# An encoder layer on one core: in the last pair of blocks, splits ahead of cross-engine steps, a fourth room for down parts, own room for T4's high part

## The reference

```
x += concat(A, B) @ W_out            (windowed attention A, conformer convolution B)
h2 = RMSNorm(x)
g = silu(dwconv3(h2 @ W_gate) + b)   (1024 -> 2816, a convolution of three taps along the tokens)
y = x + (g * (h2 @ W_up)) @ W_down   (2816 -> 1024)
```

## Time and profile before

| | us |
|---|---|
| median of 3 runs | 2765.27 (2764.12 to 2770.18) |
| the profiled execution | 2761.62 |
| its span, first to last instruction | 2759.8 |
| PE busy | 2683.6 (97%) |
| PE weight loads busy | 2325.1 (84%) |
| DVE busy | 1809.7 (66%) |
| ACT busy | 1241.6 (45%) |
| mean granted PE clock | 0.996 |

### The profile page before, as it was taken

The page is one execution under the profiler, slowest core; times in us unless marked ns, Lnnn a source line. Parts: engine busy times, 40 slices in busy tenths (PEclk is TensorE's granted clock), DMA queues, the critical chain, the costliest instruction groups (busy, mean ns, idle before and its releaser), DMA issues. The chain is left out here.

```text
span 2759.8 us, 34848 instructions
## 1 busy us (share of the span) xinstructions
PE 2683.6 (97%) x13056; PEld 2325.1 (84%) x13056; DVE 1809.7 (66%) x2995; ACT 1241.6 (45%) x2003; POOL 194.9 (7%) x334
## 2 busy tenths in 40 slices
PE   7999999999999999999999999999999999999997
PEld 5677777788888898888898888888899999999997
DVE  3664656688567877577877577876267565765663
ACT  5344463466535446436446345446144333433432
POOL 0100012200110000110000110000000000000001
PEclk9999999999999999999999999999999999999999
DMA  9866759843563443753543753434744412222212
GB/s 306 294 221 229 259 192 344 292 141 108 205 235 129 154 138 109 267 202 108 164 131 111 294 175 117 154 127 141 281 160 166 149 58 58 65 63 58 64 47 68
DMA packets 138919, 454.22 MB, mean 165 GB/s; under 512 B 24480, under 2 KB 37152, under 8 KB 122112
## 3 DMA queue, kind: packets, MB, share of 16 engines
q1 hardware_dynamic: 111616, 349.16, 37.5%
q0 software_dynamic: 27136, 102.84, 10.4%
HBM read 363.15 MB, written 88.79 MB: 164 GB/s over the span
## 5 line engine op out<-in xcount | busy, mean ns | idle before, releaser
L2001 PE MATMUL bank<-hw_hi,weights 128*128 128x440 f32 (+1 forms) x2816 | 812.3, 365 | 0.0
L2001 PEld LDWEIGHTS bank<-hw_hi,weights 128*128 128x128 f32 x2816 | 530.0, 188 | 57.0 <-issue 22.4
L2001 PE MATMUL bank<-hw_lo,weights 128*128 128x440 f32 (+1 forms) x1408 | 510.8, 363 | 0.0
L2017 PE MATMUL bank<-mid,weights 128*128 128x438 f32 x2112 | 432.0, 364 | 0.0
L2017 PEld LDWEIGHTS bank<-mid,weights 128*128 128x128 f32 x2112 | 396.0, 189 | 40.5 <-issue 11.9
L1478 DVE TENSOR_TENSOR weights<-wraw,weights 128x1024 fp32r<-128x1024 f32 x286 | 348.9, 1220 | 114.7 <-ACT weights L1090 114.2
L1090 ACT ACTIVATE weights<-wraw 128x1024 fp32r<-128x1024 f32 x286 | 301.5, 1054 | 252.3 <-DMA wraw<-w_down_t 165.7
L1581 DVE SCALAR_TENSOR_TENSOR cc<-win,par,cc 128x512 f32<-128x512 f32 x600 | 414.0, 745 | 0.0
L1973 PE MATMUL bank<-h_hi,weights 128*128 128x512 f32 x1120 | 367.3, 400 | 13.8 <-DVE weights L1478 12.8
L1973 PEld LDWEIGHTS bank<-h_hi,weights 128*128 128x128 f32 x1120 | 211.7, 189 | 84.9 <-issue 37.2
L2001 PEld LDWEIGHTS bank<-hw_lo,weights 128*128 128x128 f32 x1408 | 264.4, 188 | 16.6 <-issue 1.0
(11 more groups left out here) (184 smaller groups left out, 3643.5 us busy)
## 6 DMA issues: line engine op xcount, KB each, us to landing
weights<-weight_scratch SPq DMA_DIRECT2D x88, 1024.0 KB, 5.8
wraw<-w_ffn_t SPq DMA_DIRECT2D x176, 512.0 KB, 3.4
wraw<-w_down_t SPq DMA_DIRECT2D x88, 512.0 KB, 3.5
weight_scratch<-weights POOLq DMA_DIRECT2D x22, 1024.0 KB, 7.3
part_raw<-w_ffn_t SPq DMA_DIRECT2D x88, 256.0 KB, 2.6
part_raw<-w_pass_t SPq DMA_DIRECT2D x44, 256.0 KB, 2.6
cat_hi<-cat_scratch SPq DMA_DIRECT2D x10, 1024.0 KB, 7.7
cat_lo<-cat_scratch SPq DMA_DIRECT2D x10, 1024.0 KB, 12.1
```

Source lines behind the costliest of these rows:

```text
L2001: mm = nc.tensor.matmul(out, l[:, k, :], r[:, k, 1:TC + 1] if s else r[:, k, :], start=(k == 0 and j == 0), stop=(k == KT - 1 and j == 2))
L2017: mm = nc.tensor.matmul(out, l[:, q, :], mid[:, k, part, :], start=(k == 0 and j == 0), stop=(k == FH - 1 and j == 2))
```

## The change

Four edits, all in the last pair of blocks. In each slot's list, `high` and `low` now come before `tap0`, `product` and `mid_high`; only the last `product` and `mid_high` of a pass (those of product 4, `ends_pass`) still stand ahead. The down parts have 4 rooms instead of 3, so the fourth part of a pass is split three slots ahead too, in the slot in which the pass starts. T4's high part has a room of its own, waits for no store, and is made in slot 1 (low part: slot 2). Loads of down parts follow the 4 rooms.

```diff
-HI_RING = 5
+HI_RING, DOWN_RING = 5, 4
+def ends_pass(gi):
+    return PROD[at(gi, 4) + 1][0] == "D"
 for _gi in range(ALL_GROUPS):
-    _gate = _gi % 2 == 0
     for _e, _p in enumerate((1, 5, 6)):
         ACT_AT[at(_gi, _p) + 1].append(("copy", _gi, _e))
-    for _x, _p in enumerate((2, 3, 7, 4)):
-        _t = at(_gi, _p) + 1
-        if _x < 3:
-            DVE_AT[_t].append(("add", _gi, _x))
-        if _gate:
-            ACT_AT[_t].append(("tap0", _gi, _x))
-        else:
-            DVE_AT[_t].append(("product", _gi, _x))
-            ACT_AT[_t].append(("mid_high", _gi, _x))
+    for _x, _p in enumerate((2, 3, 7)):
+        DVE_AT[at(_gi, _p) + 1].append(("add", _gi, _x))
+    if ends_pass(_gi):
+        DVE_AT[at(_gi, 4) + 1].append(("product", _gi, 3))
+        ACT_AT[at(_gi, 4) + 1].append(("mid_high", _gi, 3))
...
-    _t = max(_t, _k - (1 if PROD[_k][0] == "D" and PROD[_k][3] >= 3 else LEAD))
+    _t = max(_t, _k - (1 if PROD[_k][0] == "D" and PROD[_k][3] >= DOWN_RING else LEAD))
...
         ACT_AT[_t].append(("high", _k))
         DVE_AT[_t].append(("low", _k))
+for _gi in range(ALL_GROUPS):
+    for _x, _p in enumerate((2, 3, 7, 4)):
+        _t = at(_gi, _p) + 1
+        if _gi % 2 == 0:
+            ACT_AT[_t].append(("tap0", _gi, _x))
+        elif _x < 3 or not ends_pass(_gi):
+            DVE_AT[_t].append(("product", _gi, _x))
+            ACT_AT[_t].append(("mid_high", _gi, _x))
...
-for _d in range(3, len(DOWNS)):
-    SP_AT[DOWNS[_d - 3] + 1].append(("down", _d))
+for _d in range(DOWN_RING, len(DOWNS)):
+    SP_AT[DOWNS[_d - DOWN_RING] + 1].append(("down", _d))
...
         for _i, _b in enumerate(B_ORDER[5:]):
-            ACT_AT[5 * _i].append(("window_high", _q, _b))
-            DVE_AT[5 * _i + 1].append(("window_low", _q, _b))
+            ACT_AT[_i].append(("window_high", _q, _b))
+            DVE_AT[_i + 1].append(("window_low", _q, _b))
...
-        b_at.append(y_at[1] + Y_BYTES)
+        b_at.append(R_HW - B_BYTES)
...
-                    if b == "T4":
-                        for o in range(KT):
-                            act.wait_ge(s_yst[o], 16 * PLAIN)
```

More of the change, by code:

```diff
@@ L386 @@
 for _gi in range(ALL_GROUPS):
-    _gate = _gi % 2 == 0
     for _x, _p in enumerate((2, 3, 7, 4)):
         _t = at(_gi, _p) + 1
-        if _gate:
+        if _gi % 2 == 0:
[6 more added lines that the diff above has]
+        _t = at(_gi, _p) + 1
+        if _gi % 2 == 0:
             DVE_AT[_t + 1].append(("taps", _gi, _x))
             ACT_AT[_t + 2].append(("swish", _gi, _x))
-        elif _x == 3 and _t < PRODS and PROD[_t][0] == "D":
-            DVE_AT[_t].append(("mid_low", _gi, _x))
         else:
-            DVE_AT[_t + 1].append(("mid_low", _gi, _x))
+            DVE_AT[_t + (0 if _x == 3 and ends_pass(_gi) else 1)].append(("mid_low", _gi, _x))
 for _k in DOWNS:
@@ L565, in encoder_layer @@
         e_at = [R_D + 4 * B_BYTES + E_BYTES * i for i in range(3)]
-        w_at = [R_HW + W_BYTES * i for i in range(13)] + [W_BYTES * i for i in range(5 + HI_RING)]
+        w_at = [R_HW + W_BYTES * i for i in range(13)] + [W_BYTES * i for i in range(5 + HI_RING)] +             [R_SIDE + 8 * B_BYTES + V_BYTES]
         w_end = W_BYTES * (5 + HI_RING)
@@ L571, in encoder_layer @@
         y_at = [R_MID + M_BYTES + Y_BYTES * i for i in range(2)]
-        b_at.append(y_at[1] + Y_BYTES)
+        b_at.append(R_HW - B_BYTES)
         assert R_D + 4 * B_BYTES + 3 * E_BYTES <= R_MID and R_HW + 13 * W_BYTES <= R_SIDE
-        assert v_at[2] + V_BYTES <= R_D and b_at[13] + B_BYTES <= R_HW
+        assert v_at[2] + V_BYTES <= R_D and R_SM <= b_at[13] and y_at[1] + Y_BYTES <= b_at[13]
         b_raw, b_lo, b_hi = {}, {}, {}
@@ L587, in encoder_layer @@
         w_places = [("A", 1, a) for a in ("A11", "S1", "S2", "A12", "S4", "S3")] + [("A22", 1), ("A22", 2)] + \
-            [("D", i) for i in range(3)]
+            [("D", i) for i in range(DOWN_RING)]
         w_offset = {k: w_at[i] for k, i in w_place.items()}
@@ L610, in part_of @@
                 return part_key(GROUPS * t[1] + t[2], A_OF[t[3]])
-            return "D", DOWN_AT[k] % 3
+            return "D", DOWN_AT[k] % DOWN_RING
         def col(name, i=0):
@@ L865, in load_down @@
             def load_down(d):
-                if d < 3:
+                if d < DOWN_RING:
                     sp.wait_ge(s_used, SLOTS)
                 else:
-                    sp.wait_ge(s_used, SLOTS + DOWNS[d - 3] + 1)
-                sp.dma_start(p_raw["D", d % 3][:], w_pass[d % (len(DOWNS) // PAIRS)]).then_inc(s_rw[d % 3], 16)
+                    sp.wait_ge(s_used, SLOTS + DOWNS[d - DOWN_RING] + 1)
+                sp.dma_start(p_raw["D", d % DOWN_RING][:], w_pass[d % (len(DOWNS) // PAIRS)]).then_inc(s_rw[d % DOWN_RING], 16)
             def load_pair_y(q, i):
@@ L944, in _ @@
                 load_part(1, a)
-            for d in range(3):
+            for d in range(DOWN_RING):
                 load_down(d)
@@ L1317, in part_high @@
                     d = DOWN_AT[k]
-                    act.wait_ge(s_rw[d % 3], 16 * (TILES_IN[d % 3] + d // 3 + 1))
+                    act.wait_ge(s_rw[d % DOWN_RING], 16 * (TILES_IN[d % DOWN_RING] + d // DOWN_RING + 1))
                 else:
```

## The result

| | before | after |
|---|---|---|
| median of 4 runs each, side by side | 2766.03 (2764.12 to 2770.18) | 2745.92 (2743.65 to 2748.94) |
| ratio | | 0.9926, 95% interval 0.9909 to 0.9943 |
| the profiled execution | 2761.62 | 2748.94 |
| its span | 2759.8 | 2747.2 |
| slot 0 starts at | 2169.03 | 2180.48 |

A forecast was written before the change was run, and what follows sets the result against it. PE, busy 97%, was taken as the bound, losing 41.2 us above its pace; 16.4 left gives a gain of 24.8, so the profiled execution goes from 2761.6 to 2736.8, plus 3.7 for a median of 2740.5, range 2732 to 2751.

The forecast's parts named there:

- The loop: DVE and ACT's ping-pong in the three slots ahead of a down pass falls from 3.50 to 2.33 us a slot.
- DVE's low part waiting less than 0.5 in up groups: Sign expected in the profile after: DVE's low part, which waited 1.14 for ACT, waits under 0.5 us in up groups.
- Periods of 99.2: Sign expected in the profile after: distance between down passes of 99.2 us instead of 103.2.
- The room's cost: Fourth room puts a low part before mid_low: PE waits 1.1 in slots 48, 84, 120, 156, 2.2 in 16, 3.1 at 190.
- a stretch of slow matmuls of 1.8: Term for slots 156 to 189: one run of matmuls at lowered clock, as before the change, costing 1.8 us.
- part three: T4's earlier copies remove its wait, slow matmuls and slot 16's late entry: 5.6 us, all that slots 0 to 15 lose.
- The gate groups: Taking tap0 from in front of high there removes only pauses of about 1 us a period.
- A: Rival, chance 0.15: ahead of passes the ping-pong stays in part, gain 9 us smaller, time 2749.5.
- D: Rival, chance 0.07: order inside a slot does not matter, only T4's 5.6 is won, pass waits cost; time 2767.
- C: Rival, chance 0.02: new pauses leave PE at half clock for whole parts at each pass's start; slower, 2783.
- B: Rival, chance 0.10: all seven remaining waits bring half clock, 1.8 us each, gain 11 smaller, time 2751.5.
- The total: From slot 0 to the end, 16.4 of 41.2 us lost above PE's pace remain, a gain of 24.8.

The follow-up runs named there:

- e3: Kernel before with only the fourth room for down parts added, old order and T4 unchanged; median 2777.84, ratio 1.0030.
- e4: Changed kernel with three rooms for down parts instead of four; median 2737.81, ratio 0.9881 to the kernel before.
- e5: Changed kernel, four rooms, low of each pass's fourth part put behind that slot's mid_lows; median 2739.68, ratio 0.9894 to the kernel before.
- e2: Kernel before with only the order changed, three rooms, T4 late; median 2738.94, ratio 0.9888.
- e1: Kernel before with only T4's own room and earlier place, old order, three rooms; median 2768.48, ratio 0.9993.
- e8: Kernel before with the order changed in up groups only, three rooms, T4 late; median 2757.80, ratio 0.9961.
- e9: Kernel before with the order changed in gate groups only, three rooms, T4 late; median 2744.87, ratio 0.9916.
- e10: The changed kernel unaltered, measured and profiled a second time; median 2745.97, ratio 0.9920 to the kernel before.
- e7: e5 with the last pass's later parts split one slot ahead, its third mid_low before the fourth product, group 2's A22 loaded in slot 1; 2733.35, again 2732.84.

## Why the prediction was right, and where it was not

**The loop, right once.** 2.33 was worked out, 2.32 measured, but from the second product to the third alone; with the swish in it the first took 2.84. So DVE gains 1.3 between its first and its third product (6.50 to 5.16), where the prediction took 1.17 off each of three slots. Its sign "DVE's low part waiting less than 0.5 in up groups" did not come: in slot 44 it waits 1.16, though DVE is now early enough for PE not to wait. Periods of 99.2 were predicted all the same and three of 99.2 measured, for the reason under the gate groups; the stretch from slot 16 to slot 48 was to lose 5.1 and loses 5.2 (85.5 against 80.3).

**The room's cost, right.** 1.1 predicted for each of four passes (its own addends give 1.0), 0.9 measured; 2.2 in slot 16 and 1.96 measured; 3.1 at slot 190 and 3.10; 2.1 before product 4 of group 21 and 1.86; a stretch of slow matmuls of 1.8, and 1.5 measured: nine matmuls from 2700.10 to 2703.28, 3.18 in place of 1.67, in this window of the changed kernel (columns as above):

```profile
2700.00:2704.00 4.00, 3.90 (x13) 3.87 (x14) 0.49 (x1) 0.00 (x0) 0.00 (x0) 0.57 0.00 0
```

The 1.8 did not follow from the prediction's own row, which gives 4.4 - 2.4 = 2.0. e3, e4 and e5 confirm the cause, and sharpen it: it is the place of the low part, not the room. The room alone cost more (10.1) than inside the change (6.8). Of these 3.3, 3.0 are the clock and not waits: e3 has slow matmuls behind its 1.98 in slot 16 (5.91 from window 0 to slot 17, against 4.36 in the changed kernel), and e4, with which the change is compared, has 1.5 of them in slot 189 that the changed kernel has not.

**T4, wrong.** The step "So the wait, the slow matmuls and the late entry of slot 16 go: 5.6, all that slots 0 to 15 lose", put down to part three, failed. The 5 us are won (36.4 in place of 41.3), but the order wins most of them: e2, without T4's edit, takes 37.4 and leaves 0.43 of the wait, while e1 gets 0.8 in all from T4's edit. And 1.5 of the 5 were slow matmuls that e8 does not have behind the same wait. I had read the row's wait for T4's low part as the cost of where T4's copies stood, and not asked why DVE came to it so late.

**The gate groups, wrong in size.** "there DVE is not late enough for long waits of PE, only for pauses of about 1 us a period" is true of the waits inside these groups, but their lateness is paid in the next up group. Alone they are worth 4.2 of a period's 5.2, and the up groups, to which I gave about four fifths, 2.0. The sum came out right, since both go together in the change, and only the sum of a period was checked. The right total thus says nothing for the shares, and T4's and this one were wrong.

**The rivals.** A (the ping-pong stays in part) is false: no wait on an add within the passes' approach. D is false: e2 wins most, not T4. C is false: the new waits leave PE at half clock for eleven matmuls at most. B is half true. Of the eleven waits of 2.79 or more in the stretches of before, after, e1, e3, e8, e9 and e10 all but one (T4's in e8) have slow matmuls behind them. Of the eight waits of 1.86 to 1.98, in after, e2, e3, e4, e5 and e10, four do and four do not. Each such run of 7 to 12 matmuls at 1.2 in place of 2.4 GHz, with starts 0.34 apart in place of 0.19, costs 1.2 to 1.9 (from the lengths of the same slots with it and without). The single waits of 0.9 in the passes never did it, nor those of 1.52 to 1.58 at slots 48 to 156; in e1 1.63 and 0.86 close together did. The Trainium skill, in "TensorE: Matmul & The Clock Gate", section "A second HAM failure mode: psum-queue depth-cycling", has frequent short pauses between groups of matmuls take the clock back and forth. The traces agree for pauses of 2.79 and more in ten of eleven cases and for those of about 1.9 in half, not for those of 0.9.

**The total.** 24.8 was predicted of the stretch, 24.1 and 22.5 measured in two executions. The medians gave 20.1 and 22.8 (2768.76 to 2745.97). The median came out 5.4 above the forecast. An execution with slow matmuls in slot 16, which the sum did not have, is 1.6 longer; how many of the runs have them is not known. No term of the sum is off by the rest, which stays open, and the interval of the ratio (15.8 to 25.2 us) holds 24.8.

**A better version.** e7 is 13.1 below the changed kernel on one chip (2732.84 against 2745.97), 1.3% below the kernel before. Of the 41.2 that the stretch lost above PE's pace, about 5 are left: the three waits for y adds (2.9 from start to start), 0.9 in slot 16 and 0.8 before product 4 of group 21.

## What to carry to other kernels

When two in-order engines hand work back and forth, put what feeds the busy engine ahead of whatever waits for the other one, and count lateness over the whole chain: a group that shows no wait itself can be the one that makes the next group late. A wait on a row names who was last, not whose place is wrong; ask why that engine came late before moving the thing it was waiting for. A room more gave nothing here (e5), and cost 7 us while the instruction that fills it stood between a result and its consumer.

## What the hardware showed that was not expected

- A pause of PE of 1.86 to 1.98 is followed by half clock or not, from execution to execution of one program (1.98 with granted clock 0.68, 1.96 with 1.00, above).
- The unchanged first 2169 us differ by up to 11.5 between profiled executions (slot 0 at 2169.03 to 2180.48) while the two stretches of one program differ by 1.6 at most (566.7, 568.3 for the changed kernel). A small edit is better judged by the stretch it touches than by the span.
